# Two thirds of the down projection computed in seven-product blocks, in a two-layer decoder step on one core

## What is computed

```python
def swiglu(h, wg, wu, wd):
    return (jax.nn.silu(h @ wg) * (h @ wu)) @ wd
# per layer: x = x + swiglu(rmsnorm(x, g), w_gate, w_up, w_down);  d_model 1024, d_ff 2816
```

## Time and profile before

| what | value |
|---|---|
| runs | 2421.8, 2423.62, 2428.49 us |
| span of the profiled execution, first to last instruction | 2420.9 us |
| TensorE busy | 2349.3 us (97%) |
| VectorE, ScalarE, GpSimd busy | 1508.1, 750.4, 843.5 us |
| matmuls | 16326 |
| mean granted TensorE clock | 0.994 |

### The profile page before, as it was taken

How to read it: one execution, slowest core, us unless ns; L and a number is a source line. 1 busy time by engine, 2 the same in 40 slices (tenths; PEclk the granted TensorE clock), 3 DMA queues, 4 the chain that set the end, 5 groups by cost and what they waited for, 6 DMA issues and landing times.

```text
span 2420.9 us, 40635 instructions
## 1 busy us (share of the span) xinstructions
PE 2349.3 (97%) x16326; PEld 2276.2 (94%) x16326; DVE 1508.1 (62%) x2499; ACT 750.4 (31%) x1440; POOL 843.5 (35%) x557
## 2 busy tenths in 40 slices
PE   7899999999999999999999999999999999999998
PEld 6889999999999999999999766699999999999997
DVE  9993257555555576775534577756755555557766
ACT  4452134333333211031100377843433333320103
POOL 0003325544445443332332000043555444443431
PEclk9899999999999999999999999999999999999999
DMA  3155101222222422212256454210222222242212
GB/s 123 38 141 175 53 18 66 82 70 73 71 79 79 166 85 90 88 53 88 88 184 209 126 145 141 71 36 18 70 79 79 79 79 71 70 157 105 79 62 71
DMA packets 107540, 221.41 MB, mean 91 GB/s; under 512 B 35802, under 2 KB 59866, under 8 KB 107362
## 3 DMA queue, kind: packets, MB, share of 16 engines
q1 hardware_dynamic: 94130, 179.95, 23.3%
q10 hardware_dynamic: 13232, 38.94, 4.4%
HBM read 171.79 MB, written 44.71 MB: 89 GB/s over the span
## 4 chain that ended last, share of the span: by engine, by line
PE 84%; DVE 11%; issue 2%; ACT 1%; DMA 1%; POOL 0%; SPq 0%; DVEq 0%; ACTq 0%; POOLq 0%
PE pair L2130 45%; PE pair L2384 12%; PE pair L2387 12%; PE pair L2388 12%; PE pair L2617 1%; DVE nmx L1933 1%; DVE act_lo L1454 1%; DVE Vp L1373 1%; DMA zn<-zblk 1%; DVE wmix L2010 1%; DVE acc L1373 1%; DVE Vp L1795 1%; PE pair L2298 1%; DVE act_lo L1407 0%; DVE G_im L1373 0%
## 5 line engine op out<-in xcount | busy, mean ns | idle before, releaser
L2384 PE MATMUL pair<-act_hi,w_hi 128*128 128x344 f32 x1408 | 450.0, 320 | 6.7 <-DVE gate L1373 3.0
L2388 PE MATMUL pair<-act_hi,w_lo 128*128 128x344 f32 x1408 | 450.1, 320 | 0.0
L2387 PE MATMUL pair<-act_lo,w_hi 128*128 128x344 f32 x1408 | 449.9, 320 | 0.0
L2130 PE MATMUL pair<-act_hi,w_hi 128*128 128x344 f32 x1152 | 371.1, 322 | 2.7 <-DVE act_lo L1373 2.1
L2130 PE MATMUL pair<-act_hi,w_lo 128*128 128x344 f32 x1152 | 368.2, 320 | 0.0
L2130 PE MATMUL pair<-act_lo,w_hi 128*128 128x344 f32 x1152 | 368.0, 319 | 0.0
L732 POOL CAST w_hi<-w_raw 128x1024 fp32r<-128x1024 f32 x90 | 114.8, 1276 | 722.8 <-issue 309.5
L1373 DVE TENSOR_TENSOR X<-X,pair 128x344 f32<-128x344 f32 x528 | 252.9, 507 | 150.8 <-PE pair L2130 150.8
L2130 PE MATMUL pair<-hid_hi,w_hi 128*128 128x344 f32 x1056 | 338.2, 320 | 1.1 <-POOL w_lo L735 1.1
L2130 PE MATMUL pair<-hid_lo,w_hi 128*128 128x344 f32 x1056 | 338.5, 321 | 0.0
L2130 PE MATMUL pair<-hid_hi,w_lo 128*128 128x344 f32 x1056 | 338.0, 320 | 0.0
(11 more groups left out here) (308 smaller groups left out, 4199.7 us busy)
## 6 DMA issues: line engine op xcount, KB each, us to landing
w_raw<-w SPq DMA_DIRECT2D x180, 512.0 KB, 4.0
hid_raw<-hid SPq DMA_DIRECT2D x20, 1032.0 KB, 5.7
hid<-gate ACTq DMA_DIRECT2D x22, 516.0 KB, 2.7
hid<-gate_odd ACTq DMA_DIRECT2D x22, 516.0 KB, 2.6
kpg<-cache_k SPq DMA_DIRECT2D x16, 512.0 KB, 5.4
vpg<-cache_v SPq DMA_DIRECT2D x16, 512.0 KB, 7.0
qd<-qt SPq DMA_DIRECT2D x28, 256.0 KB, 5.4
ublk<-x_b SPq DMA_DIRECT2D x8, 576.0 KB, 8.3
```

Source lines behind the costliest of these rows:

```text
L2130: return t_.matmul(out, lhsT, rhs, start=start, stop=stop)
L2384: ins = t_.matmul(out, wh, rhs[k][0], start=first and k == 0, stop=False, skip_group_check=True)
L2387: t_.matmul(out, wh, rhs[k][1], start=False, stop=False, skip_group_check=True)
L2388: last = t_.matmul(out, wl, rhs[k][0], start=False, stop=k == HK - 1, skip_group_check=True)
```

## The change

Of the 22 hidden tiles of each layer, 16 (`FB`) are taken out of the plain loop and computed in 8 more blocks (`ND`): blocks 22 to 29, `down_block` on VectorE and ScalarE, the same `block` on TensorE. Each of them computes two output tiles from 8 hidden tiles with 132 matmuls. Four such blocks share one set of activations, so the set is replaced twice in each layer: beside block 21 for blocks 22 to 25 and beside block 25 for blocks 26 to 29 (`REFILLS`, `FRESH`). `NIT` falls from 11 to 3. A set is 6 pieces of 4x128 rows and 344 columns, loaded from `hid` as soon as the block before has read the old piece for the last time (`load_piece`), or earlier into a new tile `bst` (`load_columns`). From it come 3 sums on VectorE and one on GpSimd, 9 high parts on ScalarE, 8 low parts on VectorE and one on GpSimd. The raw piece and the low part share a place.

VectorE adds three results of a down block straight into X (`into_x`) and writes three others to SBUF, which GpSimd adds (`x_add`). In `first_down` GpSimd now makes these additions for the last block in front of and between the splits. The order of products stays: in blocks 22 and 26 too, P6, which reads T2, is third. Smaller parts: the three semaphores `x_in` become one, `y_last` is merged into `y_done`, several loads are written out instead of looped, and the scratch for dynamic DMA is set to 1024.

```diff
+FB = 16
+ND = FB // 2
+NBK = FT + ND
+NIT = (FT - FB) // 2
+REFILLS = {FT - 1: 0, FT + 3: 1}
+FRESH = {FT: 0, FT + 4: 1}
+RF_DVE = ("sum T1", "sum T2", "B11", "T1", "sum T4", "T2", "B21", "T4", "T3", "C2", "B22")
+RF_POOL = ("C1", "sum T3")
...
             def block_sums(f, b):
...
                 low_of_sum(f, b, "S3", 3)
+                if b - 1 in REFILLS:
+                    low_of_tokens(f, b - 1)
+                if b > FT:
+                    x_add(f, b - 1, 4)
                 pool.wait_ge(st_lo_a, n4 + 3)
                 g.tensor_tensor(q["A12"], q["A12"], stmp[:], ALU.add).then_inc(st_sum, 1)
+                if b - 1 in REFILLS:
+                    sum_three(f, b - 1)
+                if b > FT:
+                    x_add(f, b - 1, 7)
                 low_of_sum(f, b, "S4", 4)
...
             def first_down(f):
...
+                x_add(f, NBK - 1, 4)
+                x_add(f, NBK - 1, 7)
                 for x in range(4):
+                    if x == 1:
+                        x_add(f, NBK - 1, 8)
                     split(u, u % 4, u // 4, freed, f + 1)
...
+            def x_add(f, b, ev):
+                p = (b - FT) % HK
+                m, n, part_ = {4: (2 * p + 1, 1, tmp[:, 1, :]), 7: (2 * p + 1, 0, tmp[:, 0, :]),
+                               8: (2 * p, 1, gate[:, 1, :])}[ev]
+                pool.wait_ge(st_ev, 8 * (NBK * f + b) + ev)
+                g.tensor_tensor(X[:, m, cs(n)], X[:, m, cs(n)], part_, ALU.add).then_inc(st_add, 1)
+            def low_of_tokens(f, b):
+                r, x = turn_of(f, b), piece(act_raw, "C1")
+                pool.wait_ge(rf_hi, high_done(r, "C1"))
+                g.tensor_tensor(piece(act_lo, "C1"), x, piece(act_hi, "C1").bitcast(F32), ALU.subtract).then_inc(rf_pool, 1)
+            def sum_three(f, b):
+                r = turn_of(f, b)
+                pool.wait_ge(rf_dve, dve_done(r, "sum T1"))
+                pool.wait_ge(rf_in["S22"], rf_landed(r))
+                g.tensor_tensor(bst[:, 0], bst[:, 1], bst[:, 0], ALU.subtract).then_inc(rf_pool, 1)
...
             def block(f, b, late=None, last=None):          # VectorE
                 tt(u2, x2, p1, ALU.add).then_inc(st_ev, 1)
+                    refill_sum(f, b, "T1", "P5")
+                    refill_sum(f, b, "T2", "P6")
                     slot_low(f, b + 1, "A11")
+                    refill_low(f, b, "B11")
...
+                refill_low(f, b, "T1")
+                if b and b not in REFILLS:
                     slot_low(f, b + 1, "A21")
...
+                refill_sum(f, b, "T4", "P7")
                 dve.wait_ge(st_step, past(B, "P4"))
...
+                if b in REFILLS:
+                    slot_low(f, b + 1, "A12")
+                    refill_low(f, b, "T2")
+                else:
                     slot_low(f, b + 1, "A22")
                 dve.wait_ge(st_step, past(B, "P3"))
...
+            def down_block(f, b):                           # VectorE
+                if b in FRESH:
+                    refill_low(f, b - 1, "B21")
+                    refill_low(f, b - 1, "T4")
+                    refill_low(f, b - 1, "T3")
+                    slot_low(f, b, "A22")
+                dve.wait_ge(st_step, past(B, "P6"))
...
+                tt(u2, x2, p1, ALU.add).then_inc(st_ev, 1)
+                refill_low(f, b - 1, "C2")
...
             def block(f, b, w, beside):                     # TensorE
+                fresh, r = b in FRESH, turn_of(f, b - 1)
                 for name in order(b):
+                    if fresh and name in ("P1", "P5", "P6", "P2", "P7", "G2", "P4", "P3"):
+                        piece_of = {"P1": "B11", "P5": "T1", "P6": "T2", "P2": "B21", "P7": "T3", "G2": "C2", "P4": "T4",
+                                    "P3": "B22"}
+                        pe.wait_ge(rf_dve, dve_done(r, piece_of[name]))
+                    if fresh and name == "G1":
+                        pe.wait_ge(rf_pool, pool_done(r, "C1"))
```

More of the change, by code:

```diff
@@ L317, in build @@
         blk_in = sem("blk_in")
-        x_in = [sem(f"x_in{n}") for n in range(NC)]
+        x_in = sem("x_in")
         w_in = [sem(f"w_in{r}") for r in range(4)]
@@ L468, in hid_loads, with piece, raw_of @@
             return 16 * (f * (NIT + 1) // 2 + i // 2 + 1 + i % 2)
+        PIECE = {"B11": (0, 0), "T1": (0, 1), "C1": (0, 2), "B21": (HK, 0), "B22": (HK, 1), "C2": (HK, 2)}
+        def piece(x, name):
+            k, n = PIECE[name]
+            return x[:, k:k + HK, cs(n)]
+        def raw_of(name):
+            return {"T2": mixed_f[:, 4:8, :], "T3": bst[:, 0], "T4": mixed_f[:, 14:18, :], "B22": bst[:, 1]}.get(name)
         def attention_steps(eng, step):
@@ L801, in blocks @@
             def blocks(f):
-                for b in range(FT):
+                for b in range(NBK):
                     block_sums(f, b)
@@ new lines, in block @@
+                refill_high(f, b, "B11")
+                slot_high(f, b + 1, "A11")
+                refill_high(f, b, "T1")
+                for name in ("S2", "A21"):
+                    slot_high(f, b + 1, name)
+                refill_high(f, b, "T2")
+                silu(f, b, 0)
+                slot_high(f, b + 1, "S3")
+                refill_high(f, b, "C1")
+                slot_high(f, b + 1, "A12")
+                silu(f, b, 2)
+                refill_high(f, b, "B21")
+                slot_high(f, b + 1, "A22")
@@ L970, in block @@
+                refill_high(f, b, "T4", "P4")
+                silu(f, b, 1)
+                slot_high(f, b + 1, "S4")
+                refill_high(f, b, "T3")
+            def down_block(f, b):
+                B, more = NBK * f + b, b + 1 < NBK
+                first_product(B)
+                refill_high(f, b - 1, "C2")
+                if b == FT:
+                    store_hidden(f, FT - 1)
+                refill_high(f, b - 1, "B22", "P3")
+                if not more:
                     first_high(f, 0)
-                silu(B, 0)
@@ L972, in block @@
-                if not more:
                     first_high(f, 1)
-                if more:
-                    slot_high(f, b + 1, "S3")
-                    slot_high(f, b + 1, "A12")
-                silu(B, 2)
-                if more:
-                    slot_high(f, b + 1, "A22")
-                silu(B, 1)
-                if more:
-                    slot_high(f, b + 1, "S4")
+                    return
+                slot_high(f, b + 1, "S1")
+                refill_high(f, b, "B11")
@@ L1002, in ffn @@
                     block(f, b)
+                for b in range(FT, NBK):
+                    down_block(f, b)
                 hidden_high(f, 1)
-                store_hidden(FT * f + FT - 1)
                 for i in range(2, NIT):
@@ L1551, in block @@
                 tt(G[:, 2, :], cg, R[:, cs(2)], ALU.mult).then_inc(st_ev, 1)
-                if more:
+                if b not in REFILLS:
                     slot_low(f, b + 1, "A12")
@@ L1921, in ffn @@
                     block(f, b)
+                for b in range(FT, NBK):
+                    down_block(f, b)
+                dve.wait_ge(st_add, 3 * ND * (f + 1))
                 for i in range(NIT - 1 - f):
```

308 lines of the change are left out of this document (227 added, 81 removed).

## The result

The changed kernel takes 2462.68 us, the median of 4 runs (2461.46 to 2463.71), beside 2423.89 us for the kernel before on the same chip: 1.0159 times as long (95% interval 1.0145 to 1.0174). The forecast was 2462.

What follows compares the result with a forecast made beforehand. TensorE, busy for 97% of the span, was taken as the bound. Matmuls -30.2, refill waits +47, hand-over +15.8 and clock +6.6 gave +39 us: span 2460, median 2462 us, range 2436 to 2490.

Steps and rivals of the forecast that it cites:

- 96 fewer matmuls: On TensorE, 1056 matmuls replace 1152 per layer; 192 fewer in two layers at 0.1573 us each, -30.2 us.
- clock, and restart after waits: TensorE's clock falls after waits over 2.94 us; two counted per layer, 1.65 us each, +6.6 us, bounds 0 and 13.
- hand-over: Before the plain down matmuls, TensorE waits 7.9 us per layer for GpSimd's additions and splits; +15.8 us.
- The common line: VectorE operations on two SBUF operands and GpSimd operations exclude each other; blocks 21 and 22 ask 55.3 of 41.5 us.
- The rival in which the operations pass each other: At the refills, long VectorE and GpSimd operations do not hinder each other, so no waits; 2412 us, chance 0.11.
- the one in which GpSimd wins: GpSimd comes first at each tie with whole-length holding; 29 to 37 us per layer in the refills, 2492 us, chance 0.14.
- the third: Rival: demand slips further as VectorE finds gaps, each refill costs 5 us; 2434 us, chance 0.07.
- The variant in which the line is held to the very end of an operation: Refills, first come first served, whole operations held: 31 us per layer, 2478 us, chance 0.15 within the forecast's own.
- The 58 us: Upper bound of refill waits, 2 x 29, with holding to each operation's end and GpSimd first at ties.
- The walk: Engine queues followed in written order through the refills; TensorE waits 14.4 plus 9.1 us per layer, +47 us in two layers.
- four GpSimd operations get between them: In block 22, GpSimd operations intervene among VectorE's T4, T3 and A22 before u2, so P7 waits 5.6 us.
- the demand count: Line time asked in the refill blocks less time available and 5.0 us slipping onward; floor 8.8 + 8.4 = 17.2 us per layer.

Runs made afterwards that it cites:

- e3: Changed kernel with GpSimd's two refill operations taken out (memset for C1's low part, no T3 sum); 2449.08 us, ratio 1.0093 to the kernel before.
- e10: Changed kernel with e1, e6 and e7 combined, A22's low part moved as in e11, other refill operations reordered, T3's sum earlier; 2429.88 us, ratio 1.0026.
- e6: Changed kernel with A22's and B22's low parts later in VectorE's order in blocks 22 and 26; 2470.84 us, ratio 1.0190 to the kernel before.
- e11: Changed kernel with only A22's low part moved behind the last eviction of blocks 21 and 25; 2463.76 us, ratio 1.0165 to the kernel before.
- e1: Changed kernel with GpSimd's three additions for the last block moved behind the first two down splits; 2444.29 us, ratio 1.0075 to the kernel before.
- e2: Changed kernel with product P6 fifth instead of third in blocks 22 and 26; 2465.37 us, ratio 1.0165 to the kernel before.
- e7: Changed kernel with B11's raw piece loaded early into its own tile and T1, T2 summed before u2; 2461.10 us, ratio 1.0158.
- e12: e10 with GpSimd's T3 sum and C1's low part moved to VectorE, B22's low part before A21's in blocks 22 and 26; 2414.54 us, ratio 0.9956.

## Why the prediction came out right

The number was right, in part by luck: two of its terms were wrong in opposite directions. Per layer; the measured column is the first layer of the profiled execution:

| step | forecast | measured |
|---|---|---|
| 96 fewer matmuls | -15.1 | -15.1 (20.77 us per undisturbed block) |
| waits in the refills | 23.5 | 17.8 shown as waits |
| clock, and restart after waits | 3.3 | 24.55 - 17.8 = 6.7 in the refills, 1.4 at the hand-over |
| hand-over | 7.9 | 7.75 |
| sum | 19.6 | 18.6 |

Two layers make 37.2 us by the right column (the second layer's refills lost 24.8 us, 0.3 more), and the span grew by 39.1.

- **Matmuls.** Right; nothing else came of them.
- **The common line.** Right in kind. The rival in which the operations pass each other is excluded by e3's two pairs of rows, and the one in which GpSimd wins by the size of the result. Refills of 12 us exclude the third, which gave them 5. The variant in which the line is held to the very end of an operation, with 31 us per layer, is not what the trace shows: VectorE's 3.66 us operation above needs 0.68 us and ends at 832.35, so it began 0.13 us before GpSimd's recorded end at 831.80. The 58 us that the prediction called its upper bound for two layers was no bound, since two layers of this variant make 62. VectorE's 1376 elements took 1.58 us alone (1.57 said), a piece landed in 4.3 us (5.0 said). GpSimd's took 3.43 to 3.45 in the first refill, but both start 0.4 us before the end of a VectorE operation on SBUF; alone they take 3.17 (3.1 said), as here in e10:

```profile
832.28 3.17 POOL L890 TENSOR_TENSOR act_lo<-act_raw,act_hi 128x1376 fp32r<-128x1376 f32 x1
```

- **The walk was off by 5.7 us per layer.** P6 of block 22 waited 3.49 (3.8 said), P2 1.59 (1.8), P4 1.50 (1.8) and P4 of block 21 0.79 (0.8). The step that failed is "four GpSimd operations get between them" in front of u2: P7 waited 2.23 and not 5.6. After 845.05 GpSimd stood idle for 5.58 us, for A22's low part, and got no more in; I had overlooked that wait. It cost P7 nothing. In block 26 the same wait, of 3.20 us, held up u3 by the circle that e6 shows; with A22's low part made earlier (e11) P4 of block 26 waited 0.41 us and not 3.13.
- **The clock was under-sized,** 6.6 us said, and 6.5 and 8.2 measured in the two layers. I counted one fall in two waits, 1.65 us each. The records show falls behind waits of 2.23, 2.86, 3.13 and 7.59 us, each followed by 1.4 to 1.7 us of lost work, while the 3.49 us wait, which should have had one by that reckoning, left it at 1.00 in the first layer; in the second it fell behind that wait too.
- **The hand-over** was worked out from the queue and hit; e1 gave all of it back.
- **The start** gave 2.1 us that no step had. u2 of block 0 ended its wait at 382.17 before and 384.28 after, but in the eleven experiments, whose code up to there does the same work, it lies anywhere from 379.68 to 386.92. So the 2.1 us cannot be told from scatter between executions, and that the span grew by the very 39 us of the forecast is luck to that extent.
- **Place or amount?** Both, in this order. Of moves that left the line's work alone, e2, e7 and e11 changed nothing that can be told and e6 lost 8 us; all together, with 3.3 us more room (e10), brought the refills from 24.6 to 17.6 us per layer, which is where the demand count had put the floor. From there, some 7 us less line time brought 7.9. That both steps land within 0.4 us of the count is better than its terms deserve: with 3.17 us for GpSimd's operation, e12 takes 2 x 3.2 and not 2 x 3.7 us of line time off, which gives 10.8 and not 9.8, and the 5.0 us that slip into the next block were an estimate. That demand sets a floor is supported by e3, by e12 and by e10's full line; its exact height is not shown, and e12 also moved the operations to other places in the queues.

So the change as made loses because each refill costs about 12 us where 8 hidden tiles save 7.6, and because 9.2 us per layer go at the hand-over. With the hand-over mended, a refill has to cost under 7.6 us; e12's cost 5.6 and 4.2.

## What to carry to other kernels

Before moving work into half-idle engines, count what they ask of the path that they share, in the blocks where the work falls and not over the span: 55 us asked of 41.5, less the 5 that the next block could take, came close to what the best order still cost, while VectorE's 62% over the span said nothing. When an engine goes through a fixed queue, read first what stands ahead of an operation that others need: three additions in front of two splits cost 18 us, and moving them behind the splits gave that back with the same work. Reordering alone moves a wait to its neighbour until the circle of waits is known; list for each engine what it idles for, not only what TensorE waits for.

## What the runs showed of the hardware

- A GpSimd memset that only writes (1376 elements, 1.24 us) did not hold up a VectorE operation with two SBUF operands (0.68 us under it), whereas a GpSimd subtraction of the same size stretched the same operation to 3.66.
- The clock did not follow the length of the last wait. It stayed at 1.00 around a single 3.49 us wait at 839 and fell around 2.23 us at 851, after two other waits and TensorE busy for only 2.16 of the 5 us from 845 to 850. In e1_handover, with the same code and nearly the same waits up to there, it fell behind that same 3.49 us wait (at 840.59) and not behind the 2.23 us one (at 852.47):

```profile
836.00:841.00 5.00, 1.51 (x10) 1.00 0.00 0
841.00:846.00 5.00, 5.00 (x24) 0.66 0.02 3
```

So the length of the waits alone does not tell where it falls; what decides is not shown. In the refills of the changed kernel it was at 0.50 for about 3.4 us each time, and at the hand-over for about 6.8, of which TensorE worked through the last 2.8.
